# A depthwise convolution by constant spectral transforms, with tokens on partitions, in a two-block transformer kernel on one core

## What is computed

```python
CONV_WIDTH = 31
LN_EPS = 1e-5

def conformer_conv(x, w_pw1, b_pw1, w_dw, b_dw, ln_g, ln_b, w_pw2, b_pw2):
    h = x @ w_pw1 + b_pw1
    a, gate = jnp.split(h, 2, axis=-1)
    h = a * jax.nn.sigmoid(gate)
    h = lax.conv_general_dilated(
        h, w_dw[:, None, :].astype(h.dtype),
        window_strides=(1,), padding=[(CONV_WIDTH - 1, 0)],
        dimension_numbers=('NWC', 'WIO', 'NWC'),
        feature_group_count=D_MODEL) + b_dw
    h = jax.nn.silu(layer_norm(h, ln_g, ln_b))
    return h @ w_pw2 + b_pw2
```

## Time and profile before

| | before |
|---|---|
| median of 3 runs | 1332.92 us (1332.46 to 1334.28) |
| span of the profiled execution, first to last instruction | 1330.2 us |
| TensorE busy | 98% of the span |
| VectorE busy | 66% |
| ScalarE busy | 47% |
| GpSimd busy | 8% |
| mean granted TensorE clock | 0.998 of full |

### The profile page before, as it was taken

How to read it: one execution, slowest core, us unless ns; L and a number is a source line. 1 busy time by engine, 2 the same in 40 slices (tenths; PEclk the granted TensorE clock), 3 DMA queues, 4 the chain that set the end, 5 groups by cost and what they waited for, 6 DMA issues and landing times.

```text
span 1330.2 us, 17856 instructions
## 1 busy us (share of the span) xinstructions
PE 1306.7 (98%) x7374; PEld 1130.3 (85%) x7374; DVE 873.8 (66%) x988; ACT 625.0 (47%) x760; POOL 100.3 (8%) x141
## 2 busy tenths in 40 slices
PE   7999999999999999999999999999999999999997
PEld 5888877888888888899888888998888887988886
DVE  5565676767677655886777755557775566777753
ACT  5255576524455533325455543345554355455540
POOL 4123011001000002110000000000000010100000
PEclk9999999999999999999999999999999999999999
DMA  9544535456656655310455574545556422565540
GB/s 317 164 165 162 178 127 154 163 191 198 211 181 194 209 192 195 127 64 1 159 172 190 188 235 165 190 159 186 190 188 228 159 96 83 186 218 190 186 166 32
DMA packets 164911, 224.82 MB, mean 169 GB/s; under 512 B 7473, under 2 KB 105857, under 8 KB 164832
## 3 DMA queue, kind: packets, MB, share of 16 engines
q1 hardware_dynamic: 163168, 220.23, 50.3%
q0 software_dynamic: 1648, 3.47, 1.0%
q10 hardware_dynamic: 16, 0.00, 0.0%
HBM read 222.62 MB, written 1.05 MB: 168 GB/s over the span
## 4 chain that ended last, share of the span: by engine, by line
PE 94%; DVE 3%; ACT 2%; DMA 0%; issue 0%; POOLq 0%; DVEq 0%; POOL 0%; SPq 0%; ACTq 0%
PE acc L652 14%; PE acc L595 14%; PE acc L597 14%; PE acc L596 14%; PE att L652 8%; PE acc L650 7%; PE att L650 4%; PE att L891 4%; PE acc L626 2%; PE acc L630 2%; PE acc L628 2%; PE tp L673 1%; ACT pre L1310 1%; DVE wlo L1384 1%; ACT whi L1092 0%; DVE wexp L1938 0%
## 5 line engine op out<-in xcount | busy, mean ns | idle before, releaser
L1384 DVE TENSOR_TENSOR wlo<-raw,whi 128x2048 fp32r<-128x2048 f32 x208 | 474.6, 2290 | 167.9 <-ACT whi L1092 167.8
L1092 ACT ACTIVATE whi<-raw 128x2048 fp32r<-128x2048 f32 x208 | 395.0, 1913 | 102.4 <-PE acc L597 92.2
L652 PE MATMUL acc<-aT,whi 128*128 128x512 f32 x832 | 290.9, 391 | 0.0
L650 PE MATMUL acc<-aT,wlo 128*128 128x256 f32 x832 | 233.6, 281 | 0.0
L652 PEld LDWEIGHTS acc<-aT,whi 128*128 128x128 f32 x832 | 155.6, 187 | 33.8
L595 PE MATMUL acc<-whi,aT 128*128 128x512 f32 x448 | 179.6, 401 | 3.7 <-DVE wlo L1384 2.0
L597 PE MATMUL acc<-wlo,aT 128*128 128x512 f32 x448 | 175.8, 392 | 0.0
L596 PE MATMUL acc<-whi,aT 128*128 128x512 f32 x448 | 175.7, 392 | 0.0
L652 PE MATMUL att<-aT,whi 128*128 128x512 f32 x448 | 157.8, 391 | 0.0
L650 PEld LDWEIGHTS acc<-aT,wlo 128*128 128x128 f32 x832 | 157.3, 189 | 0.0
L595 PE MATMUL acc<-whi,hT_hi 128*128 128x512 f32 x352 | 137.3, 390 | 0.0
(11 more groups left out here) (306 smaller groups left out, 1737.7 us busy)
## 6 DMA issues: line engine op xcount, KB each, us to landing
raw<-in_ffn_w_gate_dram SPq DMA_DIRECT2D x88, 512.0 KB, 3.8
raw<-in_ffn_w_up_dram SPq DMA_DIRECT2D x88, 512.0 KB, 4.9
raw<-in_ffn_w_down_dram SPq DMA_DIRECT2D x88, 512.0 KB, 4.7
raw<-in_w_in_dram SPq DMA_DIRECT2D x72, 512.0 KB, 4.6
raw<-in_conv_w_pw_dram SPq DMA_DIRECT2D x24, 512.0 KB, 4.7
raw<-in_w_kv_dram SPq DMA_DIRECT2D x16, 512.0 KB, 5.0
raw<-in_ret_w_o_dram SPq DMA_DIRECT2D x8, 512.0 KB, 4.8
raw<-in_diff_w_o_dram SPq DMA_DIRECT2D x8, 512.0 KB, 4.4
```

Of the source, the lines that this page charges most:

```text
L650: mm_(bank[:, 0:T], wlo[:, slot, cols], aT_hi[:, kt, :], start=half == 0 and j == 0, stop=False, skip_group_check=True)
L652: last = mm_(bank[:, :], whi[:, slot, cols], aT[:, kt, :, :].rearrange("p a n -> p (a n)"), start=False, stop=half == 1 and j == SLAB_K - ...
L1092: A_(whi[:, slot, :], raw[:, slot, :], ACT.Copy).then_inc(hi_ready, 1)
L1384: V.tensor_tensor(wlo[:, slot, :], raw[:, slot, :], whi[:, slot, :].bitcast(F32), ALU.subtract)\
```

## The change

The convolution is computed through a spectrum. 30 tokens of history and 128 own tokens make a window of 158 tokens. Its real Fourier transform is kept in 236 rows: real part, imaginary part and their sum for each of 78 frequencies, and two rows for the frequencies that are real. A product of two spectra is then elementwise in these rows, and the way back is linear. All transforms are constant matrices (`table`, 512 KB, computed on the host when the program is built and loaded from HBM by one DMA), so that they are plain fp32 matmuls with tokens as the contraction:

- `analyse_taps`: the spectrum of the taps, 8 matmuls of 31 rows and 256 columns, in four row groups of the array.
- `analyse(c)`: the spectrum of 256 channels of both token blocks, 6 matmuls of 256 columns; the third of each three adds the last 32 tokens of block 0 as history of block 1.
- `multiply(c)`: two DVE products out of PSUM.
- `make_tokens(t, n)`: back to tokens, 2 matmuls of 512 columns; the bias of the convolution comes in as one more row.

The result has tokens on partitions in PSUM. The layer norm becomes a row norm: `bn_stats` and `bn_aggr`, a scale and a shift for each token, then 16 transposes, and SiLU with gain and bias out of PSUM. pw2 then runs token block by token block: all of block 0 first, in the `att` banks, then block 1. The parity split, `pick`, `flip`, `matrices`, `convolve`, `mean_of`, the pivot, the folds, the filler matmuls and the copies to `uT` are gone. The casts and remainders of pw2's slabs 2 and 3 move: both casts to right after pw1, the remainder of slab 2 ahead of `glu_bias(3)`, that of slab 3 in between the two blocks' norms. The tile `gain` has 96 columns instead of 128, so that all tiles allocated behind it move by 128 bytes.

```diff
-FOLD = 12
-EARLY_SLABS = (5, 9)
-KEEP_WARM = 22
...
+HIST = TAPS - 1
+WINDOW = P + HIST
+SPEC_A = P
+SPEC_B = 3 * (WINDOW // 2 - 1) + 2 - SPEC_A
+SPEC_COLS = 2 * P
...
+def spectrum_table():
...
+    own = np.arange(P) + HIST
+    for r, (k, part) in enumerate(spec):
+        table[:, r] = analyse(k, part, own)
+        table[P - HIST:, SPEC_COLS + r] = analyse(k, part, np.arange(HIST))
+        for q in range(4):
+            table[32 * q:32 * q + TAPS, 2 * SPEC_COLS + r] = analyse(k, part, HIST - np.arange(TAPS))
...
+        co, si = np.cos(angle) / WINDOW, np.sin(angle) / WINDOW
+        back = co if k in (0, WINDOW // 2) else 2 * {"re": co + si, "im": si - co, "sum": -si}[part]
+        half, row = divmod(r, P)
+        table[row, 3 * SPEC_COLS + half * P:3 * SPEC_COLS + (half + 1) * P] = back
+
+    table[SPEC_B, 3 * SPEC_COLS + P:] = 1.0
+    return table.astype(np.float32)
+
...
+NG = len(GAINS) * KT
...
+        u = sb("u", [P, TT, D], to=conv)
+        spec = sb("spec", [P, 2, TT, D], to=conv)
+        tap_spec = sb("tap_spec", [P, 2, D], to=conv)
+        yn = sb("yn", [P, TT, D], to=conv)
...
+            pool.dma_start(table[:, :], spectrum).then_inc(taps_landed, 16)
+            for q in range(4):
+                pool.dma_start(taps[32 * q:32 * q + TAPS, :], A["conv_w_dw_2"][0][:, q * (D // 4):(q + 1) * (D // 4)])\
+                    .then_inc(taps_landed, 16)
...
             for t in range(TT):
...
+                pool.dma_start(spec[SPEC_B:SPEC_B + 1, 1, t, :], A["conv_b_dw_2"][0:1, :]).then_inc(taps_landed, 16)
+            nc.gpsimd.memset(ln_eps[:, :], LN_EPS).then_inc(pad_ready, 1)
...
+            pool.wait_ge(ystat_ready, 2)
+            own(nc.gpsimd.tensor_scalar(ydev[:, 1:2], ymv[:, 1, 1:2], 1.0, LN_EPS, ALU.mult, ALU.add))
+            nc.gpsimd.tensor_tensor(yrs[:, 1:2], ydev[:, 1:2], mhalf[:, 0:1], ALU.pow).then_inc(yrs_ready, 1)
...
+            def analyse_taps():
+
+                pe.wait_ge(taps_landed, 16 * 7)
+                for half, rows_ in ((0, SPEC_A), (1, SPEC_B)):
+                    for q in range(4):
+                        at = slice(32 * q, 32 * q + TAPS)
+                        last = mm_([att, tp][q // 2][q % 2][0:rows_, half * T:(half + 1) * T],
+                                   of_taps[at, half * P:half * P + rows_], taps[at, :], start=True, stop=True)
+                last.then_inc(tap_mm, 1)
+
+            def analyse(c):
...
-            def convolve(i):
-
...
-                for d_ in range(SHIFTS):
-                    last = mm_(att[i % 2][:, 0:P], wm[:, i % WM_BUFS, d_ * P:(d_ + 1) * P],
-                               uT[:, i, PADN - d_:PADN - d_ + P], start=d_ == 0, stop=d_ == SHIFTS - 1)
-                last.then_inc(conv_mm, 1)
...
+                if c < 2:
+                    pe.wait_ge(tap_done, 4)
+                else:
+                    pe.wait_ge(prod_done, 2 * (c - 1))
+                banks = [att, tp][c % 2]
+                cols = slice(c * FW, (c + 1) * FW)
+                halo = slice(P - 32, P)
+                for half, rows_ in ((0, SPEC_A), (1, SPEC_B)):
+                    to = slice(half * P, half * P + rows_)
+                    mm_(banks[half][0:rows_, 0:FW], own_tokens[:, to], u[:, 0, cols], start=True, stop=True)
+                    mm_(banks[half][0:rows_, FW:CW], own_tokens[:, to], u[:, 1, cols], start=True, stop=False)
+                    last = mm_(banks[half][0:rows_, FW:CW], last_tokens[halo, to], u[halo, 0, cols],
+                               start=False, stop=True)
+                last.then_inc(fwd_mm, 1)
...
+            def make_tokens(t, n):
+
+                cols = slice(n * CW, (n + 1) * CW)
+                mm_(y_banks(t)[n][:, :], back[:, 0:P], spec[:, 0, t, cols], start=True, stop=False)
+                mm_(y_banks(t)[n][:, :], back[0:SPEC_B + 1, P:2 * P], spec[0:SPEC_B + 1, 1, t, cols],
+                    start=False, stop=True).then_inc(inv_mm, 1)
...
+            def transpose_y(t, n):
+
+                pe.wait_ge(normed, 2 * t + n + 1)
+                if t == 1:
+                    pe.wait_ge(siluc, 4 * n + 4)
+                for j in range(4):
+                    kt = 4 * n + j
+                    last = nc.tensor.transpose(tp[n][:, j * P:(j + 1) * P], yn[:, t, kt * P:(kt + 1) * P], ident[:, :])
+                last.then_inc(yn_tr, 1)
...
+            def pw2_part(t, c, half, kts):
+
+                k = p2a.k + 2 * half + c
+                for kt in kts:
+                    pe.wait_ge(silo, KT * t + kt + 1)
+                    one = [pw2_banks[tt][c] for tt in range(TT)]
+                    last = part(one, aT_hi, aT_lo, k % SLOTS, kt % SLAB_K, (kt,), t, kt == 0, kt == KT - 1)
+                return last
...
-                slab(p1.k + s, p1.g + c, half, aT_hi, aT_lo, phase)
+                slab(p1.k + s, p1.g + c, half, aT_hi, aT_lo)
...
-                    pe.wait_ge(pad_ready, CONV_CONSTS)
-                    pe.wait_ge(rs_ready, RS_MIXA + 1)
-                    for t in range(TT):
-                        for t2 in range(TT):
-                            last = mm_(att[1][:, t:t + 1], pick[:, t, t2, :], rs[:, RS_MIXA, t2:t2 + 1],
...
-                    for i in range(CGS):
...
-            for _ in range(KEEP_WARM):
-                mm_(att[0][:, 0:P], meanw[:, :], meanw[:, :], start=True, stop=True)
...
+                    analyse_taps()
+                if s in (4, 5):
+                    analyse(s - 4)
...
+            analyse(2)
+
+            analyse(3)
+            pe.wait_ge(prod_done, 8)
+            pe.wait_ge(acc_free, 2 * (p1.g + 3) + 2)
+            make_tokens(0, 0)
+            make_tokens(0, 1)
+            make_tokens(1, 0)
+            transpose_y(0, 0)
+            make_tokens(1, 1)
+            transpose_y(0, 1)
+
+            for half in range(2):
+                for kt in range(4 * half, 4 * half + 4):
+                    for c in range(2):
+                        if kt == 4 * half:
+                            pe.wait_ge(lo_ready, p2a.k + 2 * half + c + 1)
+                        last = pw2_part(0, c, half, (kt,))
+                        if kt == KT - 1:
+                            last.then_inc(pw2_early, 1)
+                if half == 0:
+                    transpose_y(1, 0)
+                    transpose_y(1, 1)
+
+            pw2_part(1, 0, 0, range(0, 4)).then_inc(half_done, 2)
+            pw2_part(1, 0, 1, range(4, 8)).then_inc(pw2_left, 1)
+            pw2_part(1, 1, 0, range(0, 4)).then_inc(half_done, 4)
+            exit_fills(p2a.b, p2a.g, 0)
+            pw2_part(1, 1, 1, range(4, 8)).then_inc(half_done, 2)
             ffn_pe("ffn2a")
...
+                if s == 3:
+
+                    act.wait_ge(tap_mm, 1)
+                    for half, rows_ in ((0, SPEC_A), (1, SPEC_B)):
+                        for q, pair in enumerate((att_pair, tp_pair)):
+                            A_(tap_spec[0:rows_, half, q * CW:(q + 1) * CW].rearrange("p (b n) -> p b n", n=T),
+                               pair[0:rows_, :, half * T:(half + 1) * T], ACT.Copy).then_inc(tap_done, 1)
                 cast(p1.k + s + AHEAD)
-            fill_copy(p1.b + 2, uT[:, 8:10, PADN:])
+            cast(p2a.k + 2)
             glu_sigmoid(3)
+            cast(p2a.k + 3)
...
+            act.wait_ge(pad_ready, 1)
+            act.wait_ge(ystat_ready, 1)
+            A_(ydev[:, 0:1], ymv[:, 0, 1:2], ACT.Sqrt, bias=ln_eps[:, 0:1]).then_inc(dev_ready, 1)
             nc.scalar.preload_act_table_set("silu_and_others")
...
+            def conv_silu(t, kt):
+
+                act.wait_ge(yn_tr, 2 * t + kt // 4 + 1)
+                g_, b_ = GROW["ln_g"] + kt, GROW["ln_b"] + kt
+                A_(yT[:, kt, t * P:(t + 1) * P], tp[kt // 4][:, (kt % 4) * P:(kt % 4 + 1) * P], ACT.Silu,
+                   scale=gain[:, g_:g_ + 1], bias=gain[:, b_:b_ + 1]).then_inc(siluc, 1)
...
+            def conv_high(t, kt):
+
+                act.wait_ge(siluc, KT * t + kt + 1)
+                cols = slice(t * P, (t + 1) * P)
+                A_(aT_hi[:, kt, cols], yT[:, kt, cols], ACT.Copy).then_inc(silh, 1)
+
+            for t in range(TT):
+                conv_silu(t, 0)
+                for kt in range(KT):
+                    if kt + 1 < KT:
+                        conv_silu(t, kt + 1)
+                    conv_high(t, kt)
+            cast(p2a.k + 2 + AHEAD)
+            exit_hi(p2a.b, 0, "ffn2a")
+            cast(p2a.k + 3 + AHEAD)
...
+                                           rs[:, RS_MIXA, t:t + 1], pbias[:, c, :], ALU.mult, ALU.add)\
...
+                    V.tensor_tensor(u[:, t, c * FW:(c + 1) * FW], pre[:, c % 2, t, 0:FW], pre[:, c % 2, t, FW:CW],
                                     ALU.mult).then_inc(glu_done, 1)
...
+            def multiply(c):
+
+                dve.wait_ge(fwd_mm, c + 1)
+                if c == 0:
+                    dve.wait_ge(tap_done, 4)
+                cols = slice(c * FW, (c + 1) * FW)
```

(120 more changed lines are left out.)

289 lines of the change are left out of this document (40 added, 249 removed).

## The result

| | before | after |
|---|---|---|
| median | 1333.1 us (4 runs, 1332.46 to 1334.28) | 1292.93 us (4 runs, 1291.84 to 1293.15) |
| ratio, 95% interval | | 0.970 (0.9686 to 0.9713) |
| span of the profiled execution | 1330.2 us | 1290.1 us |
| pw1's first matmul | 502.4 | 504.9 |
| module, pw1 to ffn2a's first matmul | 141.6 us | 93.8 us (predicted 91.7) |

A forecast was written before the change was run, and what follows sets the result against it. TensorE, busy 98%, was taken as the bound. Summed module terms put ffn2a's first matmul at 594.1 instead of 644.0: 49.9 us off the 1330.2 span, 1280.3, plus 2.7 gives 1283.0 us; range 1279 to 1292.

The forecast's parts named there:

- What comes after it is the same work in both kernels: From ffn2a's first matmul at 644.0 to the end, the work was taken as the same in both kernels.
- Rival 3: Down projections' 1056 matmuls slow from 0.2267 to 0.2333 because tiles behind `gain` move 128 bytes: 7 us, 1290; chance 0.04.
- Rival 1: Chain across engines is longer; PE waits for DVE at 556 to 561 and 564 to 567: about 1288; chance 0.15.
- rival 2: Clock falls in the new waits of 1.5 and 0.7 us, about 2 us a fall; two give 1287; chance 0.08.
- pw1: First projection of the module: 192 matmuls at 0.2267 instead of 0.2333, 43.5 us, as the parity stride goes.
- The taps: Spectrum of the taps inside pw1: 8 matmuls in four row groups, 1.8 us, with ends 0.9 and 3.4.
- `analyse` at 2.6: Each token spectrum: six plain fp32 matmuls of 256 columns at 0.43, 2.6 us.
- The tightest place: Before `analyse(3)`: DVE's chain of 16.5 us ends at 556.8, PE arrives at 556.4, within 0.4 us.
- Waits and pw2: PE idles 1.5 us before the first `make_tokens`, 0.7 before block 0's transposes; SiLUs in pw2 are hidden.
- rival 5: Gain is given back in ffn2a because its weights are late; no chance of its own, counted under Rival 1.
- Block 1's norm: Under pw2's first half, GpSimd's power beside DVE's 2.3 us remainder; PE waits at most 0.3 for eight transposes.
- Rival 4: Clock falls at the first wait and stays at 1.2 GHz; 60 us at half rate give 1343; chance 0.01.

## Why the prediction was right or wrong

**The step that failed** is "What comes after it is the same work in both kernels", with its mate ahead of the module: the point 502.4 was taken over from before. Both put the effect of the moved tiles at nothing. The work is the same, its speed is not, because all tiles behind `gain` moved: behind the module it took 691.4 us instead of 686.2, ahead of it 2.5 more. Rival 3 named this mechanism, its place (1056 matmuls) and its price: 7 us by the earlier trace rows against the earlier trace rows, and 6.8 and 6.7 were measured. What was wrong is its chance of 0.04, and with that the range, whose top at 1292 held rivals 1 and 2 but nothing stacked on rival 3. "No row shows that an address matters" was true and was read as if it spoke against the rival. The rows showed that two matmuls of the same shape differ by 3% by how their stationary operand lies in memory, and that was reason to leave it open. Without the shift the time is 1286.2, inside the range. That is still 3.2 over the forecast, by the two terms below: the analyses and the fall of the clock.

**pw1.** 0.2267 per matmul without the parity stride: right, so 1.3 us were gained as worked out. The taps: 1.8 taken, 1.07 measured (first start 522.52, next fp32r matmul 523.59). Eight in 1.07 against 0.43 each is 3.2 times, nearer to the lower end of 0.9 than to my choice. The Trainium skill, "TensorE: Matmul & The Clock Gate", Part 3, gives 3.07 times for four 32-row tiles, measured there with 512 columns. The trace comes close with its 3.2, and the estimate of 1.1 worked out from that figure was the better term.

**`analyse` at 2.6** was mis-sized: it takes 3.15, or 3.35 right behind another. The row is a price between matmuls of equal row count; one with another count than the one before took 0.61 to 0.63. This and the slower restart are 2.8 us, shown by the run with 128 rows. Less the 0.7 that the taps gave back, and with 0.3 for the slower first `make_tokens`, that makes 2.4; the module's error is 2.1, so all waits and crossings together came out 0.3 below their sum.

**The tightest place**, DVE and PE both at `analyse(3)` within 0.4: PE did not wait, so the chain of 16.5 us over DVE, summed from the earlier trace rows, was in time. PE had been pushed back by the slow analyses, but with 128 rows it didn't wait either (`analyse(3)` starts at 558.60, when the last matmul before it, of 0.43, ends). Rival 1 fell.

**Waits and pw2.** 1.5 and 0.7 were predicted, 1.38 and 0.74 measured; `make_tokens` 1.7, measured 1.72, 1.98 right behind the wait. ffn2a's slabs were not late (rival 5 fell), and the 512 KB table landed in 5.6 us, in time. Block 1's norm was given as hidden, "GpSimd's power is done beside the remainder". It was not: GpSimd's first instruction ended only with the remainder, the power came behind it, and DVE waited 0.74 for it. PE still waited only 0.16 because pw2's first half covered it. The Trainium skill, "SBUF — State Buffer", section "Who interferes with whom", states that a VectorE instruction with two inputs in SBUF contends with a GpSimd instruction that reads SBUF. Here 2.12 against 0.19 agrees with it; I had not weighed it.

**The clock** (rival 2). It fell in most executions, once, for 1.0 to 1.7 us, so its chance of 0.08 was too low. The profiled execution of after is the one without a fall, so its page shows 1.00 everywhere. The lower mean clock of the other three points to a fall in them, and the profile with the old `gain` shows where it fell there and for how long. The 2 us that priced it were read from slow matmuls at the kernel's start, which show no fall: the transposes ahead of them were slow too (1.97 us for eight records, 1.37 in the module of after), and the granted clock reads 1.00 there. That the price came out near is luck. Rival 4 fell: the clock was back at full within 4 us.

## What to carry to other kernels

When a small tile changes size, keep the addresses of the tiles behind it (pad it), and compare the spacing of matmuls that the change doesn't touch. Price a matmul by a row with the same neighbours, not only the same shape: a short contraction between full ones saved nothing and cost 0.2 us each way. Where TensorE waits, reorder the work so that some that is due anyway falls into the wait, and look where the wait moves to before calling it gone.

## What the runs showed of the hardware

- An fp32r matmul of 512 columns at the granted clock 1.00 starts every 0.2267 or 0.2333 us depending on where tiles lie in SBUF, most likely its stationary operand: moving them by 128 bytes cost 6.7 us in this kernel, by 256 nothing, by 64 about 2.4, the last two in one execution each.
- A plain fp32 matmul of 256 columns takes 0.43 behind one of the same row count, 0.61 to 0.63 behind one of 32 rows or as one of 32 rows behind 128.
- The granted clock read 0.61 and 0.54 in the 4 us after PE had stood still for 1.38 us in one profiled execution, whose mean clock of 0.997 the other three share. With the same wait it was 1.00 in the profiled executions of three other kernels. Waits of 0.75 and 0.79 were followed by 1.00.
- A GpSimd instruction on one column took 2.12 us beside a remainder on VectorE, 0.32 beside two short subtractions, 0.19 with neither.
